# Asking for the later sample caches in the attention's block instead of the projection's

## The reference, cut to what matters

```python
def _mem_kv(mem, w_kv, kn_g):
    B = mem.shape[0]
    k, v = jnp.split(mem @ w_kv, 2, axis=-1)
    return _rms_norm(k.reshape(B, N_MEM, H_X, HD_X), kn_g), v.reshape(B, N_MEM, H_X, HD_X)

def _mem_attend(h, mk, mv, w_q, qn_g, w_o):
    B, L, _ = h.shape
    q = _rms_norm((h @ w_q).reshape(B, L, H_X, HD_X), qn_g)
    s = jnp.einsum('blhd,bmhd->bhlm', q.astype(F32), mk.astype(F32)) * (HD_X ** -0.5)
    p = jax.nn.softmax(s, axis=-1)
    o = jnp.einsum('bhlm,bmhd->blhd', p, mv.astype(F32)).astype(h.dtype)
    return o.reshape(B, L, H_X * HD_X) @ w_o
# D_MODEL 1024, 4 heads of 128 (H_X, HD_X), N_MEM 256, DEC_BATCH 8, DEC_SEQ 8, DEPTH 2
# prompt: mk, mv = _mem_kv(mem, ...); samples: mk, mv = st['mem_k'][l], st['mem_v'][l]
```

## Time and profile before

| | |
|---|---|
| median of 3 runs | 3379.21 us |
| profiled execution | 3380.08 us |
| its span (first to last instruction) | 3378.3 us |
| TensorE busy | 3088.4 us, 91% |
| VectorE, GpSimd, ScalarE busy | 1558.7, 1058.3, 531.7 us |
| mean granted TensorE clock | 0.935 |
| memory traffic over the span | 52 GB/s |

### The profile page before, as it was taken

The page is one execution under the profiler, slowest core; times in us unless marked ns, Lnnn a source line. Parts: engine busy times, 40 slices in busy tenths (PEclk is TensorE's granted clock), DMA queues, the critical chain, the costliest instruction groups (busy, mean ns, idle before and its releaser), DMA issues. The chain is left out here.

```text
span 3378.3 us, 43932 instructions
## 1 busy us (share of the span) xinstructions
PE 3088.4 (91%) x18135; PEld 2937.9 (87%) x18135; DVE 1558.7 (46%) x1786; ACT 531.7 (16%) x874; POOL 1058.3 (31%) x551
## 2 busy tenths in 40 slices
PE   7997668899999999999988879689979999999999
PEld 6987468789999999998977769469869999999999
DVE  4152454256626436256114444663446634626343
ACT  3111122152000000002111021351252000000000
POOL 3332033114334334343320142103203434434342
PEclk9998679999999999999986789789989999999999
DMA  3111121401111111113100111011221111111112
GB/s 117 44 31 38 24 90 56 142 24 50 45 48 44 39 49 40 47 38 99 41 19 14 46 56 38 15 67 49 87 101 47 48 40 50 37 50 44 44 44 80
DMA packets 274509, 175.86 MB, mean 52 GB/s; under 512 B 15262, under 2 KB 261406, under 8 KB 274398
## 3 DMA queue, kind: packets, MB, share of 16 engines
q1 hardware_dynamic: 274398, 174.29, 16.9%
HBM read 158.00 MB, written 16.27 MB: 52 GB/s over the span
## 5 line engine op out<-in xcount | busy, mean ns | idle before, releaser
L327 PE MATMUL psum<-moving_hi,w_hi 128*128 128x384 f32 (+1 forms) x3888 | 1285.4, 331 | 71.9 <-PEq L515 24.9
L328 PE MATMUL psum<-moving_lo,w_hi 128*128 128x384 f32 (+1 forms) x3888 | 1279.3, 329 | 0.0
L329 PE MATMUL psum<-moving_hi,w_lo 128*128 128x384 f32 (+1 forms) x3888 | 1279.3, 329 | 0.0
L289 POOL TENSOR_TENSOR w_hi<-w_raw,one 128x1024 fp32r<-128x1024 f32 (+2 forms) x236 | 407.1, 1725 | 1934.2 <-PE psum L329 1390.3
L327 PEld LDWEIGHTS psum<-moving_hi,w_hi 128*128 128x128 f32 x3888 | 739.6, 190 | 79.9 <-issue 63.7
L328 PEld LDWEIGHTS psum<-moving_lo,w_hi 128*128 128x128 f32 x3888 | 739.8, 190 | 0.5 <-issue 0.5
L329 PEld LDWEIGHTS psum<-moving_hi,w_lo 128*128 128x128 f32 x3888 | 739.1, 190 | 0.0
L294 POOL TENSOR_TENSOR w_lo<-w_raw,w_hi 128x1024 fp32r<-128x1024 f32 (+2 forms) x236 | 574.0, 2432 | 18.5
L368 DVE TENSOR_TENSOR residual<-psum,residual 128x768 f32 x192 | 130.1, 719 | 491.9 <-PE psum L329 491.2
L327 PE MATMUL psum<-hidden_hi,w_hi 128*128 128x384 f32 (+1 forms) x1056 | 344.6, 326 | 3.2 <-DVE hidden_lo L1900 3.2
L329 PE MATMUL psum<-hidden_hi,w_lo 128*128 128x384 f32 (+1 forms) x1056 | 345.1, 327 | 0.0
(11 more groups left out here) (292 smaller groups left out, 2862.5 us busy)
## 6 DMA issues: line engine op xcount, KB each, us to landing
w_raw<-in_ffn_w_gate SPq DMA_DIRECT2D x44, 512.0 KB, 3.8
w_raw<-in_ffn_w_up SPq DMA_DIRECT2D x44, 512.0 KB, 3.8
w_raw<-in_ffn_w_down SPq DMA_DIRECT2D x48, 384.0 KB, 3.1
w_raw<-in_od_w_in SPq DMA_DIRECT2D x22, 512.0 KB, 3.9
w_raw<-in_ev_w_in SPq DMA_DIRECT2D x20, 512.0 KB, 3.7
w_raw<-in_mem_w_kv SPq DMA_DIRECT2D x16, 512.0 KB, 3.6
work_h<-in_cache_mem_kT SPq DMA_DIRECT2D x4, 2048.0 KB, 12.3
work_h<-in_cache_mem_v SPq DMA_DIRECT2D x4, 2048.0 KB, 17.0
```

What stands on the lines that cost most here:

```text
L289: nc.gpsimd.tensor_tensor(hi, raw, ONE.to_broadcast([P, kt * P]), ALU.mult).then_inc(own.sem, 1)
L327: pe.matmul(out, sh, mh, start=(k == 0), stop=False)
L328: pe.matmul(out, sh, ml, start=False, stop=False)
L329: return pe.matmul(out, sl, mh, start=False, stop=(k == kt - 1))
```

## The change

In the projection block SyncE asks only for the caches of the first four sequences, and it asks for chunk 11 between their keys and their values. The caches of the later four sequences are asked for by SyncE at the beginning of the attention's block, ahead of its two stores. The semaphores on which the second sample unit waits are the same.

```diff
-def _attend(nc, g, units, scale, room, turned_last=None, keep=()):
+def _attend(nc, g, units, scale, room, turned_last=None, keep=(), fetch=()):
...
         if keep:
             @block.sync
             def _(sp):
+                for dst, src, arrives in fetch:
+                    sp.dma_start(dst, src).then_inc(arrives.sem, 16)
                 for dst, src in keep:
                     g.store(sp, dst, src)
                 sp.wait_ge(g.stored.sem, g.stored.at(g.stores[0]))
...
                 for c in range(2, 11):
                     fetch(c)
                 sp.wait_ge(full.sem, full.at(8))
-                for bt in range(2):
-                    (kd, ks), (vd, vs) = caches(bt)
-                    sp.dma_start(kd, ks).then_inc(keys_in[bt].sem, 16)
-                    sp.dma_start(vd, vs).then_inc(values_in[bt].sem, 16)
-                    if bt == 0:
-                        fetch(11)
+                (kd, ks), (vd, vs) = caches(0)
+                sp.dma_start(kd, ks).then_inc(keys_in[0].sem, 16)
+                fetch(11)
+                sp.dma_start(vd, vs).then_inc(values_in[0].sem, 16)
                 for c in range(2):
                     sp.wait_ge(w_split.sem, w_split.at(11 + c))
                     sp.dma_start(g.slot(g.WRAW[c], 4), w_o[0](c, c, 0)[0]).then_inc(w_loaded[c].sem, 16)
...
     run(_attend, nc, g, [prompt_unit(j) for j in range(NBLK)] + [sample_unit(0, 0), sample_unit(1, 1)], HD_X ** -0.5, CST,
-        turned_last=(turn_samples, place_samples),
+        turned_last=(turn_samples, place_samples), fetch=[(dst, src, arrives[1]) for (dst, src), arrives in zip(caches(1), (keys_in, values_in))],
```

## The result

The changed kernel takes 3348.1 us (median of 4 runs, 3346.81 to 3349.52) against 3379.53 us; the ratio is 0.9907, 95% interval 0.9893 to 0.9921. The profiled execution took 3348.07 us, 32.0 us less than the one before.

A forecast was written before the change was run, and what follows sets the result against it. TensorE bounds the kernel, waiting at the attention's start for a late w_o load; 8.95 + 8.29 us of waits and 3.8 of clock make 21.0, so 3358.2 us from the runs' median; range 3353 to 3364.

The forecast's parts named there:

- What bounds the place: End of the projection block, both layers: a late 256 KB w_o load, not arithmetic; TensorE waits 10.64 and 9.60 us.
- The load of w_o: Projection block, layer 0: first w_o chunk lands near 658.4 instead of 670.86; bounds 655.3 to 659.8.
- What is late next: Block's end: VectorE's copy of the values is last, 664.35 in layer 0; waits shrink by 8.95 and 8.29 us.
- The later caches: Attention's start: moved loads cost nothing, 29 us of cover before the last unit's scores; contention -0.5 to +0.5 us.
- The clock at the attention's start: First scores: a 1.7 us pause keeps the clock, saving 1.9 us in each layer; bounds 0 and 2 x 2.5.
- The count of transfers: SyncE's loads and stores at the edited place: only their order changes, the same ten transfers are made.
- the terms of the sum: Shorter waits of 8.95 us in layer 0 and 8.29 in layer 1, plus 1.9 us of clock each: 21.0 us.
- The step that failed: After the attention block: nothing waits for a load's absolute time, so all of the 21.0 us reaches the end.
- rival (b): After the edited place: later clock falls land otherwise, one or two more or fewer, 3352 to 3365 us; chance 0.15.

The follow-up runs named there:

- order-only kernel: Kernel before with only chunk 11's load moved ahead of the first values, all caches still in the projection block: 3378.0 us (0.9997).
- kernel with one cache less in front: Changed kernel with the second keys put back ahead of the w_o load, only the second values moved to the attention block: 3359.7 us (0.9945).
- filled wait: Kernel before with 40 unread matmuls of 512 columns behind the last value product in both layers: 3373.0 us (0.9982).
- four delays: Extra matmuls in layer 0's feed-forward: 8 or 20 on the kernel before, 3373.0 and 3382.6 us; 12 or 20 on the changed kernel, 3358.4 and 3351.9 us.

## Why the prediction was wrong

- **What bounds the place**: right. The order-only kernel kept the wait, the kernel with one cache less in front lost half of it, the change all of it.
- **The load of w_o**: landed 648.45 + 8.8 = 657.25, 16.0 us after the first cache's issue; forecast 658.4 - 642.37 = 16.0.
- **What is late next**: VectorE's copy, as said; GpSimd was done 2.65 us ahead of it. The pause is 1.65 us in both layers (forecast 1.7). In front of chunk 11's products layer 1 gained 0.6 us where 0.38 were forecast, and layer 0 0.2 us where nothing was.
- **The later caches**: no wait. The keys landed 8.9 us after 663.25, at 672.2, and the last unit's scores ran at 698.56. VectorE's reduction took 1.22 us beside them. The second store landed at 669.13 + 10.9 = 680.0.
- **The clock at the attention's start**: kept at 1.00; 1.8 us in each layer (forecast 1.9). The reason given, the length of the pause, was not enough: with the filled wait nearly the same two pauses, 1.54 and 2.12 us around 3.69 us of scores, were followed by a fall in both layers, and 1.65 and 2.11 us in the changed kernel were not.
- **The count of transfers** in the prediction, ten a layer, is nine in both traces from the first cache to the second store; nothing rests on it.
- So the terms of the sum, 8.95 + 1.9 and 8.29 + 1.9, measured 11.03 and 10.37: 21.4 against 21.0.
- **The step that failed** is the sentence under the sum, "Nothing after the attention block waits for the absolute time of a load, so all of it reaches the end". It is true of loads, and I let it stand for the clock as well. The sum had no term for later clock falls. The shift of 11 us moved the entry of layer 1's projections and recurrence, where the clock goes up and down; these stages took 1.57 + 6.71 = 8.3 us less, and the start of layer 0's projection by w_o 1.0 us. That is rival (b), which I had given 0.15 and bounds of one or two falls, 3352 to 3365. Its mechanism was shown by the four delays; its size was too small, for the recurrence alone spent 34.1 us at 1.2 GHz instead of 51.2, the length of several falls. Why so many go together is not shown. What I held against (b), that the runs of before lie within 1.2 us, came from three runs; later ones of the same kernel took 3360.0 to 3382.0. Of the 32.0 us between the two profiled executions the forecast terms hold 21.4, later clock falls 9.2 and what lies ahead of the table 1.4. The last is within the scatter of the start: the first 405 us took 402.4 to 408.7 us in kernels that are the same there.

The Trainium skill, "TensorE: Matmul & The Clock Gate", section "What's actually happening", says that what watches TensorE is free-running, so that one kernel shows different numbers of slow matmuls at its start from run to run. The traces agree at the start, and the totals in part: layer 1's edit alone once gave 3351.5 and else 3361 to 3372. But the difference does not last. Against the clock's steps the first matmuls of the eighteen profiles are scattered by more than 1.5 us, and yet seventeen of them ask for the first cache within 0.1 us of each other (the other, with its delay, 1.56 us later), and all eighteen reach layer 1's last value chunk within 0.12 us. The scatter is taken up on the way, by the first 405 us above all, so a kernel tends to enter layer 1 at a position of its own, which is why single profiles could be compared at all.

## What to carry to other kernels

Where a block ends with a small load behind large ones on the same queue, move the large ones past it and check what is late next; that part can be worked out to half a microsecond. A saving ahead of a stage in which TensorE's clock goes up and down is worth itself plus or minus what the new entry does, and the range must hold that: here the three stages from layer 1's first projections to its last value chunk took 807.0 to 820.2 us in the eighteen profiles. To tell a change's worth from where the later falls land, compare stage lengths between the same instructions, and delay both kernels by a microsecond or two of plain work, put behind the places where the clock still moves.

## What the runs showed of the hardware

- The kernel before, rerun, took from 3360.0 to 3382.0 us, although its first three runs lay within 1.2 us.
- 0.17 us of entry turned the recurrence from 60.93 to 67.67 us (mean clock 0.72 to 0.62), and 1.4 us of additional work made the kernel before faster (3373.0 against 3378.6 us, the median of the kernel before beside it; ratio 0.9987, 0.9977 to 0.9996).
- A pause of 1.65 us with full rate around it left the clock at 1.00 each time; one of 5.76 us did not. Pauses of 1.54 and 2.12 us behind a filled wait were followed by a fall at 677.0 us, so the length of the pause alone does not decide.
- A delay of 1.56 us ahead of the value products was made good to within 0.12 us by a clock fall that did not come there (1.00 instead of 0.52).
- With the queue full, the issue of a 2048 KB transfer held SyncE for up to 8.85 us; on an empty queue it took 0.37 us.
- The caches' loads in the changed kernel, moved beside the first softmaxes, left VectorE's reduction at 1.22 us (1.23 before).
